# Eight experts' down weights fetched as two rows 128 apart per partition instead of two adjacent rows, with the transposes reading adjacent columns

## The reference, cut to what matters

```python
def swiglu(h, w_gate, w_up, w_down):
    return (jax.nn.silu(h @ w_gate) * (h @ w_up)) @ w_down

def moe_swiglu(h, w_router, w_gate, w_up, w_down):
    logits = (h @ w_router).astype(jnp.float32)
    top_val, top_idx = lax.top_k(logits, TOP_K)
    ...
    for e in range(N_EXPERTS):
        y = swiglu(h, w_gate[e], w_up[e], w_down[e])
        out = out + gates[..., e:e + 1].astype(h.dtype) * y
```

## Time and profile before

| | |
|---|---|
| three runs | 1734.6 us median, 1732.14 to 1739.15 |
| the profiled execution | 1731.6 us, its span 1729.9 us |
| TensorE matmul busy | 1688.9 us, 98% of the span |
| VectorE busy | 1392.7 us, 81% |
| ScalarE busy | 1120.9 us, 65% |
| HBM read | 476.66 MB |
| mixture of experts | from about 440 to 1374 us, 352 MB of the reads |

### The profile page before, as it was taken

How to read it: one execution, slowest core, us unless ns; L and a number is a source line. 1 busy time by engine, 2 the same in 40 slices (tenths; PEclk the granted TensorE clock), 3 DMA queues, 4 the chain that set the end, 5 groups by cost and what they waited for, 6 DMA issues and landing times.

```text
span 1729.9 us, 24649 instructions
## 1 busy us (share of the span) xinstructions
PE 1688.9 (98%) x9514; PEld 1454.4 (84%) x9514; DVE 1392.7 (81%) x1153; ACT 1120.9 (65%) x921; POOL 135.4 (8%) x148
## 2 busy tenths in 40 slices
PE   9999999999999999999999999999999899999999
PEld 8879999898878877888768887778887698889998
DVE  7576454656898999989999889998899979768675
ACT  6445344464677787777787778777778655855553
POOL 7100000000100000000000000000000018600000
PEclk9999999999999999999999999999999999999999
DMA  7446555553699899998999989999999944326551
GB/s 255 165 148 202 188 192 173 190 176 122 238 358 377 329 408 411 379 378 316 413 408 398 363 341 376 410 405 385 355 334 410 338 144 144 123 98 216 171 198 49
DMA packets 181165, 479.31 MB, mean 277 GB/s; under 512 B 11791, under 2 KB 80169, under 8 KB 166713
## 3 DMA queue, kind: packets, MB, share of 16 engines
q1 hardware_dynamic: 180185, 476.43, 74.0%
q10 hardware_dynamic: 864, 1.31, 0.3%
HBM read 476.66 MB, written 1.05 MB: 276 GB/s over the span
## 4 chain that ended last, share of the span: by engine, by line
PE 74%; DVE 13%; issue 6%; ACT 3%; POOL 2%; DMA 2%; DVEq 0%; ACTq 0%; POOLq 0%; SPq 0%
PE bank L2221 20%; PE bank L2222 20%; PE bank L2223 20%; DVE wl L1694 8%; ACT wh L1124 2%; DMA arena<-in_moe_w_down 2%; PE bank L2754 1%; PE bank L2340 1%; PE bank L2348 1%; PE bank L2341 1%; PE bank L2677 1%; POOL arena L899 1%; DVE wl L452 1%; PE bank L2752 1%; DVE arena L1827 1%
## 5 line engine op out<-in xcount | busy, mean ns | idle before, releaser
L1694 DVE TENSOR_TENSOR wl<-raw,wh 128x2048 fp32r<-128x2048 f32 x224 | 509.4, 2299 | 39.0 <-ACT wh L1124 38.5
L1124 ACT ACTIVATE wh<-raw 128x2048 fp32r<-128x2048 f32 x224 | 426.6, 1916 | 118.4 <-PE bank L2223 86.4
L452 DVE TENSOR_TENSOR wl<-raw,wh 128x2048 fp32r<-128x2048 f32 x112 | 254.8, 2292 | 64.7 <-ACT wh L445 62.6
L2221 PE MATMUL bank<-wh,xhl 128*128 128x512 f32 x768 | 302.7, 394 | 1.1 <-DVE wl L1694 0.7
L2223 PE MATMUL bank<-wh,xhl 128*128 128x512 f32 x768 | 299.3, 390 | 0.0
L2222 PE MATMUL bank<-wl,xhl 128*128 128x512 f32 x768 | 299.2, 390 | 0.0
L2221 PE MATMUL bank<-xhl,wh 128*128 128x256 f32 x944 | 268.1, 284 | 0.2 <-DVE wl L452 0.2
L2223 PE MATMUL bank<-xhl,wl 128*128 128x256 f32 x944 | 267.3, 283 | 0.0
L2222 PE MATMUL bank<-xhl,wh 128*128 128x256 f32 x944 | 267.2, 283 | 0.0
L1694 DVE TENSOR_TENSOR wl<-arena,wh 128x2048 fp32r<-128x2048 f32 x112 | 254.0, 2286 | 13.2 <-ACT wh L1124 13.0
L1124 ACT ACTIVATE wh<-arena 128x2048 fp32r<-128x2048 f32 x112 | 213.5, 1916 | 60.3 <-PE bank L2223 43.9
(11 more groups left out here) (484 smaller groups left out, 2477.9 us busy)
## 6 DMA issues: line engine op xcount, KB each, us to landing
raw<-in_moe_w_gate SPq DMA_DIRECT2D x80, 1024.0 KB, 7.8
raw<-in_moe_w_up SPq DMA_DIRECT2D x80, 1024.0 KB, 7.9
raw<-in_moe_w_down SPq DMA_DIRECT2D x64, 1024.0 KB, 8.2
arena<-in_moe_w_down SPq DMA_DIRECT2D x48, 1024.0 KB, 8.3
arena<-in_moe_w_up SPq DMA_DIRECT2D x32, 1024.0 KB, 8.6
arena<-in_moe_w_gate SPq DMA_DIRECT2D x32, 1024.0 KB, 7.1
raw<-in_w_up SPq DMA_DIRECT2D x22, 1024.0 KB, 5.2
raw<-in_gla_w_in SPq DMA_DIRECT2D x12, 1024.0 KB, 7.5
```

Of the source, the lines that this page charges most:

```text
L452: V.tensor_tensor(wl[:, i % NW, :], raw[:, i % NR, :], wh[:, i % NW, :].bitcast(F32), ALU.subtract).then_inc(lo_of[i][0], 1)
L1124: V.activation(wh[:, s, :], src, ACT.Copy).then_inc(sg("hi_moe"), 1)
L1694: V.tensor_tensor(wl[:, s, :], moe_raw(c)[0], wh[:, s, :].bitcast(F32), ALU.subtract).then_inc(lo_moe, 1)
L2221: T.matmul(o, xh, yh, start=first, stop=False)
```

## The change

A down piece is fetched with `kpn`, as the other pieces are: partition p gets rows p and p + 128 of the 256, two runs of 4096 bytes in place of one of 8192. The transposes then take block k of the activation as 128 adjacent columns in place of every second of 256. The destination in SBUF, the order of pieces, all waits, all matmuls and all roundings stay.

```diff
                 if kind == "d":
                     src = IN["moe_w_down"][0].rearrange("e f n -> (e f) n")[bass.ds(ee * FE + STEPS[j][0] + k * 256, 256), :]
-                    src = src.rearrange("(p k) n -> p k n", p=P)
+                    src = kpn(src)
```

```diff
                         for k in range(STEPS[j][1] // P):
-                            rows = eact[:, k // 2 * 256:(k // 2 + 1) * 256].rearrange("p (m two) -> p two m", two=2)[:, k % 2, :]
+                            rows = eact[:, k * P:(k + 1) * P]
                             if i == 0:
                                 ins = T.transpose(turned[:, k, :], rows, ident[:, :])
                             else:
                                 ins = T.matmul(turned[:, k, :], rows, fold[:, :], start=True, stop=True)
```

## The result

The changed kernel takes 1739.25 us (median of 22 runs, 1735.83 to 1742.41) against 1734.77 us (22 runs, 1731.72 to 1739.15): a ratio of 1.0025, 95% interval 1.0018 to 1.0033. It is 4.5 us slower, small but clear of noise. That is inside the forecast range of 1730 to 1740, at its upper edge, and outside the 1733 to 1737 that the prediction gave its own forecast.

A forecast was written before the change was run, and what follows sets the result against it. TensorE was taken to bound first halves, DMA and VectorE together second halves. Packets +2.2, transposes -1.1 and -0.8 summed to +0.3 us on 1731.6; shifted 3.0 to the median, 1735 us, range 1730 to 1740.

The forecast's parts named there:

- What bounds the kernel: Expert pairs: TensorE bounds first halves (138 us); in second halves (94 us) DMA and VectorE run at nearly the same pace.
- Packets: the rate: Down pieces at full DMA: 410 GB/s with 4096-byte runs against 423 and 419, costing 0.05 to 0.08 us more each.
- Packets: how much shows: Down pieces: hidden in first halves; 56 in second halves cost half of 4.5 us, +2.2 us.
- the ends 0 and 4.5: Packet cost in second halves: 0 if VectorE set the pace, +4.5 us if DMA alone did.
- transfers as the bound: Rival: transfers become the bound of the second halves, +4.5 - 1.1 = +3.4 us, 1738; chance 0.19.
- The signs: Profile after: 195501 packets, down windows about 410 GB/s, line 2752 loads about 140 ns, first halves 0.3 us shorter.
- Two signs of being wrong: Second-half down-piece landing well over 9.6 us, or a run of transposes shrinking by more than 0.1 us.
- The transposes: Adjacent columns: -1.1 us from 112 transposes in first halves, -0.8 us in second halves.
- the 0.8 of the second halves: Line 2754's 224 passes, 7 ns each, 1.6 us; half taken, -0.8 us, ends 0 and -1.6.
- The sum: Whole kernel: +2.2 - 1.1 - 0.8 = +0.3 us on the profiled 1731.6 us; median forecast 1735.
- the rivals: Transfers bind, 1738 (0.19); VectorE holds, 1732 (0.18); step free, 1737 (0.10); slower HBM rows, 1746 (0.07); whole load shows, 1725 (0.03).
- The rules of the Trainium skill: Line rate from 512 bytes would make the packet part 0; free float32 steps up to four, the transpose part 0.

The follow-up runs named there:

- split by halves: The change in the first expert of each pair only: 1732.99 us against 1734.51 for the kernel before; in the second only: 1740.13 us, ratio 1.0035.
- the 2048-byte runs: Kernel before with down pieces in four runs of 2048 bytes on a partition, rows in wrong order: 1748.75 us, ratio 1.0082.
- Packets alone: Kernel before with down pieces in 4096-byte runs, transposes still with a step of two: 1739.88 us, ratio 1.0039.
- the filled runs: Eight small matmuls in TensorE's wait at each second half's end: kernel before 1732.99 us, changed kernel 1735.89, 4096-byte runs without the transpose change 1736.14.
- the last run above: Kernel before with 4096-byte down runs, transposes still with a step of two, eight small matmuls in TensorE's wait: 1736.14 us against 1735.30, ratio 1.0006.
- columns only: Kernel before with transposes reading adjacent columns, 8192-byte down runs kept: 1733.47 us against 1734.81, ratio 0.9997.

## Why the prediction was right or wrong, point by point

**What bounds the kernel.** Right: two regimes, and DMA and VectorE side by side in the second halves. The split by halves (-1.5 and +5.6 us, together +4.1 against +4.5 for the whole) shows it.

**Packets: the rate.** Right. 409 GB/s for down pieces after, 410 forecast, and the 2048-byte runs landed at 386 GB/s with +14.0 us, clock included, for a forecast of 12.9 without.

**Packets: how much shows.** This was the step that failed: "I take half: +2.2 us". Packets alone measured +5.1 us, or 3.6 with the clock held by the lengths of the second halves (2.9 to 3.2 by the filled runs), against the ends 0 and 4.5. That is 0.065 us a piece, inside the 0.05 to 0.08 of the prediction: nearly the full price. The reason for half was that VectorE idles only 3.5 us. But that is slack within a half of 94 us, and what counts is which stream is late at its end. The chain after goes through two landings in a row there. The delay of 14 pieces does not have to be met by a wait at each of them; it comes out at the end, on a gate piece too, as the first second half of the last run above shows; in the next ones 0.2 to 0.4 us show some 60 us into the half. That the delay collects in the queue, whose engines never idle there, is my reading of this; no run tests it by itself. So the case that I called a rival, transfers as the bound (+3.4 us, 1738), is what happened. With half the price I cancelled it.

**The signs.** Packets, windows of down pieces, loads and runs of eight came out as written. Second halves grew by 0.6 to 1.5 us. First halves shrank by 0.2 us where the clock held, not 0.3. ScalarE's waits for gate pieces, which should have risen above 4.1 us if the transfers bind, stayed at 4.1; its waits for down pieces rose instead, from 6.5 to 15.4 us over all experts. Two signs of being wrong were named: the landing of down pieces rose to 10.4 us, 0.8 over its 9.6, and a run of 16 transposes shrank by 0.13 us, over the limit of 0.1 (eight of line 2752 by 0.08).

**The transposes.** The durations were right to within a nanosecond (a load of 141 ns for the forecast 140, a run of eight of 1.03 us, a pass of line 2754 with 192 ns). The gain of -1.9 us was too large. Alone they gave 0.5 us by the ratio (up to 2 in the interval). In the first halves the marks show 0.2 us each, 0.8 in four, for the 1.1 forecast. That the 0.8 of the second halves is there at all is shown by nothing: with columns only they take 432.1 us, in the kernel before 432.3. In the times the 0.8 is not seen when all packets are slow; differences of 1 us between sets of runs are at the edge of what these intervals resolve.

**The clock.** Missing from the prediction altogether. TensorE's wait at the end of a second half (2.14 us) was in the trace, and I had priced it only as idle time. It is also what precedes a fall of the clock, in some executions of the kernel before and in more of the changed kernel. That part is 1.0 to 1.6 us of the 4.5 by the filled runs, some 2.3 by runs of one clock, and 1.7 by the rest that 3.6 for packets and -0.8 for transposes leave. Why a fall comes in one execution and not in the next is open.

**The number.** The sum said +0.3 and +4.5 was measured. That the range held is owed to its width, which was made for the scatter of three runs and for the rivals; the forecast itself missed, on packets (by 0.7 to 1.4 us), transposes (by about 1.1) and the clock (by 1.0 to 2.3).

**The rules of the Trainium skill.** The Trainium skill ("DMA: Bandwidth & Descriptors", Specifications) has line rate from 512 bytes up: the three rates, 386, 409 and 419 to 423 GB/s, and three times in the same order, 1748.75, 1739.88 and 1734.8 us, speak against it. The Trainium skill ("SBUF — State Buffer", Door 1) has a step of up to four float32 for free: the load fell from 208 to 141 ns when the step of two went, so it was not free, though its effect on the end is small.

**The base.** I added to a profile of 1731.6 us and then shifted by 3.0 to the median. That shift was itself the clock's: 1731.6 to 1732.4 are the runs of the kernel before with a clock of 1.000.

## What to carry to other kernels

Where a stage has two streams of nearly the same pace, and one of them never idles, price every addition to that one nearly in full (3.6 of at most 4.5 us here): idle time of its neighbour does not say that half of the addition is hidden. A change can be good in one half of a loop and bad in the other, and applying it only where its cover exists (here, where TensorE is the bound) takes the gain alone, though here it is 0.2 us for each first half and in the times not clear of noise. And where TensorE waits for some 2 us between two stretches of dense work, look at the granted clock of several executions; filling the wait with small matmuls into a free bank brought 1.7 to 1.9 us here in one kernel and 2.8 to 3.4 in another.

## What the runs showed of the hardware

- DMA rate by length of the run in HBM, engines full, 1 MiB to 128 partitions: 386 to 387 GB/s at 2048 bytes, 408 to 410 at 4096, 419 to 423 at 8192.
- A weight load of a transpose, 128x128 float32, took 141 ns with adjacent columns and 208 with a step of two; the pace of the transposes changed by 10 ns only.
- On VectorE a product of 1024 float32 columns, one operand in PSUM, took 1214 ns in order and 2031 ns when both operands were read with a step of two and the result written to two blocks in turn. Which of the three accesses costs it was not separated.
- The granted clock fell to half for about 3.4 us (once 6.8) behind a wait of TensorE of 2.1 to 3.2 us at the end of dense work, at some ends and not at others, with 3.18 us among those without a fall. It fell at 10 of 28 such ends, and at none of 16 where eight small matmuls (1.95 us) stood in the wait. It cost some 1.2 us for each 0.001 of the mean clock.
